# Compressing the cached chunks inside the state-space quarters, with chunks transposed as gathered and 64-row products

## What is computed

```python
def compress(rows, pos, w1, w2):
    ...
    chunks = rows[:, :nch * CMP_STRIDE].reshape(b, nch, CMP_STRIDE, g, dh)
    w1b = w1.reshape(r, CMP_STRIDE, dh, w1.shape[-1])
    hid = jnp.einsum('ld,ldh->h', pos, w1.reshape(CMP_LEN, dh, w1.shape[-1]))
    for j in range(r):
        hid = hid + jnp.einsum('bnsgd,sdh->bngh', chunks[:, j:j + nc], w1b[j])
    return jnp.einsum('bngh,hd->bngd', jax.nn.gelu(hid), w2)
```

## Time and profile before

| what | us |
|---|---|
| median of three runs | 3692.41 |
| the profiled execution: its own time / its span | 3694.21 / 3692.4 |
| the four S5 quarters, 285.5 to 528.1 | 242.6 |
| compression of the samples, 1110.4 to 1360.0 | 249.6 |
| head norm of the compressed keys, 1360.0 to 1378.6 | 18.6 |
| move to DRAM, 1047.9 to 1055.2 | 7.3 |

### The profile page before, as it was taken

The page is one execution under the profiler, slowest core; times in us unless marked ns, Lnnn a source line. Parts: engine busy times, 40 slices in busy tenths (PEclk is TensorE's granted clock), DMA queues, the critical chain, the costliest instruction groups (busy, mean ns, idle before and its releaser), DMA issues. The chain is left out here.

```text
span 3692.4 us, 51281 instructions
## 1 busy us (share of the span) xinstructions
PE 3078.9 (83%) x19609; PEld 2920.3 (79%) x19609; DVE 1562.7 (42%) x3343; ACT 947.6 (26%) x1636; POOL 711.1 (19%) x492
## 2 busy tenths in 40 slices
PE   6894336499966974799999999996587999999999
PEld 3894224499955862699999999994576999999998
DVE  5236656167732343334414334326564343243341
ACT  3211013255512430231201111312463311111111
POOL 2210003121100011132222222325221322222221
PEclk7996656579977986699999999996698999999999
DMA  2211110300025316211111111110101111111112
GB/s 95 56 30 39 37 43 13 107 1 1 1 92 194 138 47 137 62 46 46 46 46 46 47 51 44 47 42 0 36 1 48 42 47 50 46 45 46 46 45 71
DMA packets 272919, 191.66 MB, mean 52 GB/s; under 512 B 60612, under 2 KB 264494, under 8 KB 268639
## 3 DMA queue, kind: packets, MB, share of 16 engines
q1 hardware_dynamic: 267414, 139.86, 13.2%
q0 software_dynamic: 4608, 49.29, 4.3%
q10 hardware_dynamic: 733, 0.30, 0.0%
HBM read 171.37 MB, written 22.26 MB: 52 GB/s over the span
## 5 line engine op out<-in xcount | busy, mean ns | idle before, releaser
L551 PE MATMUL ps<-xf_hi,w_hi 128*128 128x344 f32 x2352 | 756.7, 322 | 9.9 <-POOL w_lo L542 9.9
L553 PE MATMUL ps<-xf_hi,w_lo 128*128 128x344 f32 x2352 | 753.2, 320 | 0.0
L552 PE MATMUL ps<-xf_lo,w_hi 128*128 128x344 f32 x2352 | 752.5, 320 | 0.0
L542 POOL TENSOR_TENSOR w_lo<-w_raw,w_hi 128x1024 fp32r<-128x1024 f32 (+1 forms) x162 | 384.7, 2375 | 1488.1 <-ACT w_hi L538 1488.1
L551 PEld LDWEIGHTS ps<-xf_hi,w_hi 128*128 128x128 f32 x2352 | 443.6, 189 | 11.3 <-issue 11.2
L552 PEld LDWEIGHTS ps<-xf_lo,w_hi 128*128 128x128 f32 x2352 | 443.5, 189 | 0.7 <-issue 0.7
L553 PEld LDWEIGHTS ps<-xf_hi,w_lo 128*128 128x128 f32 x2352 | 443.5, 189 | 0.0
L551 PE MATMUL ps<-hid_hi,w_hi 128*128 128x344 f32 x1056 | 339.4, 321 | 0.0
L553 PE MATMUL ps<-hid_hi,w_lo 128*128 128x344 f32 x1056 | 337.6, 320 | 0.0
L552 PE MATMUL ps<-hid_lo,w_hi 128*128 128x344 f32 x1056 | 336.9, 319 | 0.0
L538 ACT CAST w_hi<-w_raw 128x1024 fp32r<-128x1024 f32 (+1 forms) x162 | 165.7, 1023 | 387.1 <-PE ps L553 383.8
(11 more groups left out here) (531 smaller groups left out, 5626.1 us busy)
## 6 DMA issues: line engine op xcount, KB each, us to landing
w_raw<-in_ffn_w_up_dram SPq DMA_DIRECT2D x44, 512.0 KB
w_raw<-in_ffn_w_gate_dram SPq DMA_DIRECT2D x44, 512.0 KB, 3.7
w_raw<-in_ffn_w_down_dram SPq DMA_DIRECT2D x32, 448.0 KB, 3.6
w_raw<-in_ffn_w_down_dram SPq DMA_DIRECT2D x16, 512.0 KB, 3.8
w_raw<-in_a_w_in_dram SPq DMA_DIRECT2D x14, 512.0 KB, 3.6
w_raw<-in_c_w_in_dram SPq DMA_DIRECT2D x10, 512.0 KB, 3.9
xt<-in_x_prompt_dram SPq DMA_DIRECT2D x8, 512.0 KB
win_rows<-in_cache_nsa_win_dram SPq DMA_DIRECT2D x8, 512.0 KB
```

Source lines behind the costliest of these rows:

```text
L542: pool.tensor_tensor(self.parts.lo[:, slot, 0:kt, :], self.raw[:, slot, 0:kt, :], self.parts.hi[:, slot, 0:kt, :].bitcast(F32), ALU.subtra ...
L551: pe.matmul(psum, w_hi, x_hi, start=(a == 0), stop=False)
L552: pe.matmul(psum, w_hi, x_lo, start=False, stop=False)
L553: ins = pe.matmul(psum, w_lo, x_hi, start=False, stop=(a == kt - 1))
```

## The change

The four quarters and the compression become one stage, `stage_s5_compress`: four quarters of 32 steps. A step transposes four 128x128 pieces of a gathered chunk as they lie (both groups in one piece, group 0 on rows 0 to 63, group 1 on rows 64 to 127), and then multiplies the pieces of the step before: eight products, each on its group's 64 rows, the two halves alternating. The pieces of S5 on PE stand at fixed steps (`AT`), in two PSUM banks of their own. The regroup copies are gone; ACT copies all transposed chunks. The gathers are 32 of 1 MB, the first two issued at the end of `stage_linear`. The turns of the next quarter are made by DVE within the quarter before, those of the first at the start of the stage.

For the space, `hT` is stored to DRAM during `stage_linear` and brought back in `stage_window_sample`, in place of the attention's output; the weight `w1g` is loaded during `stage_linear` where hT was, serves both compressions, and the layouts w1s and w1p go. The position term (32 products before, 64 now) moves to the start of the stage. `stage_index` moves ahead of the projection. The head norm of the compressed keys joins the first head norm; gates, `stage_cmp_sample` and `stage_select` move ahead of `stage_rows`, which now waits for its stores at its end.

```diff
@@ stage_linear, S5Params @@
+                    if side and m == 4:
+                        side.sync_later(sp)
...
+                if side:
+                    side.gpsimd_last(pool)
...
+        self.cin.spill(sp)
         sp.wait_ge(s_b, 80)
@@ stage_rows @@
-                if not first:
-                    sp.wait_ge(s_store, 16 * len(stores))
+                sp.wait_ge(s_store, 16 * len(stores))
+class CompressInputs:
...
+    def spill(self, sp):
+        sp.dma_start(self.k.d_h, self.k.hT[:, :, :].rearrange("p f t -> p (f t)")).then_inc(self.s_spill, 16)
...
+    def gather(self, pool, v):
+        b, h, half = v // 4, v // 2 % 2, v % 2
+        pool.indirect_dma_start(self.X[v % NXC][:, :], None, self.table,
+                                bass.IndirectOffsetOnAxis(ap=self.idx[:, h, half, b:b + 1], axis=0)).then_inc(self.s_in[v % NXC], 16)
...
+AT = dict(Q0=1, Q1=2, KM=3, Q2=4, Q3=5, SEC_ODD=7, X0=9, X1=10, X2=11, XS0=12, XS1=13, Y0=18, Y1=19, YS=20, SEC_EVEN=25)
+STEPS = 32
@@ stage_s5_quarter becomes stage_s5_compress: PE @@
+                def products(n):
...
+                    pe.wait_ge(s_xT, n + 1)
+                    for a in range(4):
+                        for g in range(2):
+                            rows = slice(g * HD, (g + 1) * HD)
+                            ins = pe.matmul(sums(2 * kv + g)[:, h * P:(h + 1) * P], w1g[rows, kv, 8 * half + 4 * four + a, :],
+                                            xT[rows, n % NXT, a, :], start=(half == 0 and four == 0 and a == 0),
+                                            stop=(half == 1 and four == 1 and a == 3))
...
+                for q in range(n_q):
+                    for m in range(STEPS):
+                        n = q * STEPS + m
+                        transposes(n)
+                        if n:
+                            products(n - 1)
+                        for name in at_step(m):
+                            if (name, q) in where:
+                                other(name, q)
@@ ACT @@
+                        act.copy(xT[:, n % NXT, :, :], k.ps[:, n % 2, :].rearrange("p (a n) -> p a n", a=4)).then_inc(s_xT, 1)
+                        if n % 16 == 0 and n:
+                            half_sums(n // 16 - 1)
+                        if q and m == 0:
+                            by_step(q)
+                        if m == AT["SEC_EVEN"] - 1:
+                            gelu(2 * q)
+                        if q and m == AT["SEC_ODD"] - 1:
+                            gelu(2 * q - 1)
@@ DVE @@
+                turns(0)
+                for q in range(n_q):
...
+                    combine(V, r7, wb1, i7, wb2, ALU.add)
+                    dve.sem_inc(s_v, 1)
+                    if q:
+                        hidden(2 * q - 1)
...
+                    if q + 1 < n_q:
+                        turns(q + 1)
+                    hidden(2 * q)
+                    rows_out("SEC_EVEN", q)
@@ stage_window_sample @@
-                sp.dma_start(*move).then_inc(s_moved, 16)
+                sp.dma_start(k.hT[:, :, :].rearrange("p f t -> p (f t)"), k.d_h).then_inc(s_moved, 16)
```

More of the change, by code:

```diff
@@ L1027, in _, with stage_rows @@
                     pool.tensor_tensor(t, t, root[:, j % 4, 0:w], ALU.mult).then_inc(s_done, 1)
-def stage_rows(k, kv, tok, stok, stores, first=None):
+def stage_rows(k, kv, tok, stok, stores):
     nc = k.nc
@@ L1777, in stage_s5_quarter, with at_step, stage_s5_compress, bank @@
+AT = dict(Q0=1, Q1=2, KM=3, Q2=4, Q3=5, SEC_ODD=7, X0=9, X1=10, X2=11, XS0=12, XS1=13, Y0=18, Y1=19, YS=20, SEC_EVEN=25)
+STEPS = 32
+def at_step(n):
+    return [name for name, step in AT.items() if step == n]
+def stage_s5_compress(k, s, uT, cin, posb, kc, vc):
     nc = k.nc
-    g0 = qd * QG
     NU = NC + NB
+    n_q = 4
+    n_units = 4 * NB
+    names = list(AT)
+    others = [(name, q) for q in range(n_q) for name in names if not (name == "SEC_ODD" and q == 0)] + [("SEC_ODD", n_q)]
+    where = {x: n for n, x in enumerate(others)}
+    by_act = [name[0] in "QY" or name == "KM" for name, _ in others]
+    def bank(name, q):
+        return k.ps[:, 6 + where[name, q] % 2, :]
+    def done(name, q):
+        return where[name, q] + 1
+    def out_count(n):
+        return sum(1 for m in range(n + 1) if by_act[m] == by_act[n])
+    def copied(name, q):
+        return out_count(where[name, q])
@@ L1795, in stage_s5_quarter @@
[L1795 to L1799, removed]
+        ys = k.at("y_samples", [CG, QG, NB], k.h_at + (2 * 16 * P + 2 * 8 * 4 * HD) * 4)
@@ L1815, in _ @@
[L1815 to L1851, removed]
@@ new lines, in _, with half_sums @@
+                act.wait_ge(s_hz, 1)
+                def half_sums(b):
+                    for x in range(4):
+                        act.wait_ge(s_us, 16 * b + 12 + 2 * (x // 2) + 2)
+                        if b:
+                            act.wait_ge(s_hid, 4 * (b - 1) + x + 1)
+                            act.wait_ge(s_w2, 2 * b)
+                        act.copy(h1s[:, x, :], sums(x)[HD:P, 1:256]).then_inc(s_h1, 1)
+                        act.copy(hid[:, x, 0:255], sums(x)[0:HD, 0:255]).then_inc(s_h1, 1)
@@ new lines, in gelu, with other @@
+                def gelu(b):
+                    for x in range(4):
+                        act.wait_ge(s_hid, 4 * b + x + 1)
+                        if b == 0 and x == 0:
+                            act.wait_ge(s_posb, 1)
+                        act.activation(hid[:, x, :], hid[:, x, :], ACT.Gelu_apprx_tanh,
+                                       bias=posb[:, x // 2:x // 2 + 1]).then_inc(s_gelu, 1)
+                def other(name, q):
+                    n = where[name, q]
+                    if not by_act[n]:
+                        return
+                    src = bank(name, q)
+                    act.wait_ge(s_ps, n + 1)
+                    if name in ("Q0", "Q1", "Q2", "Q3"):
+                        x = int(name[1])
+                        dst = (Q, Q2)[x // 2][:, 4 * (x % 2):4 * (x % 2) + 4, :]
+                        if q and x < 2:
+                            act.wait_ge(s_g, q)
+                        ins = act.copy(dst, src.rearrange("p (g m) -> p g m", g=4))
+                    elif name == "KM":
+                        if q:
+                            act.wait_ge(s_T, 16 * 36 * q)
+                        ins = act.copy(km[:, :], src[:, 0:P])
+                    elif name == "YS":
+                        ins = act.copy(ys[:, :, :], src[0:CG, 0:QG * NB].rearrange("p (g b) -> p g b", b=NB))
+                    else:
+                        x = int(name[1])
+                        ins = act.copy(Y[:, 4 * x:4 * x + 4, :], src.rearrange("p (g n) -> p g n", g=4))
+                    ins.then_inc(s_free_a, 1)
@@ new lines, in by_step @@
+                def by_step(q):
+                    if q:
+                        act.wait_ge(s_fin, q)
+                    act.copy(ur[:, :, :], uT[:, q, 0:T].rearrange("p (n j) -> p j n", j=L)).then_inc(s_ur, 1)
+                by_step(0)
+                for q in range(n_q):
+                    for m in range(STEPS):
+                        n = q * STEPS + m
+                        act.wait_ge(s_tr, n + 1)
+                        if n >= NXT:
+                            act.wait_ge(s_us, n - NXT + 1)
+                        act.copy(xT[:, n % NXT, :, :], k.ps[:, n % 2, :].rearrange("p (a n) -> p a n", a=4)).then_inc(s_xT, 1)
[7 more added lines that the diff above has]
+                            gelu(2 * q - 1)
+                        for name in at_step(m):
+                            if (name, q) in where:
+                                other(name, q)
@@ L1853, in _ @@
+                half_sums(NB - 1)
+                gelu(NB - 1)
             @block.vector
@@ L1873, in _ @@
[L1873 to L1885, removed]
@@ new lines, in turns @@
+                def turns(q):
+                    g0 = q * QG
+                    link(dve.memset(cos[:, :, 0:1], 1.0))
+                    link(dve.memset(sin[:, :, 0:1], 0.0))
+                    for level in range(7):
+                        m = 2 ** level
+                        cc, cs = (bc(s.turns[:, level, n, g0:g0 + 1], [[1, QG], [0, m]]) for n in (0, 1))
+                        lo_c, lo_s, tmp = cos[:, :, 0:m], sin[:, :, 0:m], t1[:, :, 0:m]
+                        hi_c, hi_s = cos[:, :, m:2 * m], sin[:, :, m:2 * m]
+                        link(dve.tensor_tensor(hi_c, lo_c, cc, ALU.mult))
+                        link(dve.tensor_tensor(tmp, lo_s, cs, ALU.mult))
+                        link(dve.tensor_tensor(hi_c, hi_c, tmp, ALU.subtract))
+                        link(dve.tensor_tensor(hi_s, lo_c, cs, ALU.mult))
+                        link(dve.tensor_tensor(tmp, lo_s, cc, ALU.mult))
+                        link(dve.tensor_tensor(hi_s, hi_s, tmp, ALU.add))
@@ L1966, in stage_s5_states @@
+                hidden(NB - 1)
+                rows_out("SEC_ODD", n_q)
 def stage_s5_states(k, s):
```

(16 more changed lines are left out.)

604 lines of the change are left out of this document (288 added, 316 removed).

## The result

The changed kernel takes 3512.88 us, median of four runs (3508.92 to 3518.85), against 3689.76 us for the kernel before in four runs: a ratio of 0.9523, 95% interval 0.9502 to 0.9544. The forecast was 3535 us, 3482 to 3625. The profiled execution has a span of 3511.5 us and a mean granted clock of 0.904 (0.877 before).

What follows compares the result with a forecast made beforehand. A chain bounds the mixer's quarters, PE most of the compression, one after the other: 492 us. Merged, 94 + 3 x 74 + 10 + 8 = 334 us, 158 less; the rest about +1: 3535 us, range 3482 to 3625.

Steps and rivals of the forecast that it cites:

- The direction and the place: Whole kernel: 157 us less, with 158 us less in the merged stage and about 1 us more elsewhere.
- One step: Merged stage on PE: 1.33 us of work plus 0.23 for two mode changes, 1.56 us a step.
- a full drain: Mode changes on PE: 0.17 us twice a step, 1.68 us instead of 1.56, 15 us more over 128 steps.
- The waits for ACT: Each quarter, PE waiting for ACT: 3.5 us at the start, 2 in the middle, 2 at gelus, together 7.5.
- The 17 us for the mixer's pieces: Each quarter on PE: mixer's records 12.4 us, with second products, YS and mode changes 17 us.
- Start and tail: Merged stage's ends: 26 us until PE can pass its second step, about 10 us behind the last step.
- The 8 us for a cold clock: Merged stage after PE's first wait: 8 us added, as eight records take 2.08 us cold, 0.89 warm.
- The chain fits: Mixer's chain within a 74 us quarter: fits, with 4 us to spare at Y and 6 at the end.
- The rest: Outside the merged stage: -5.4 head norm, -1.4 move, +5.5 stage_rows, +2 projection and barrier, about +1 us.
- the slow clock's rival: Merged stage: clock stays low, steps take 3.1 us, stage 587 us, 3790 us in all; chance 0.06.

Runs made afterwards that it cites:

- two-step experiment: Changed kernel with two steps' transposes, then two steps' products, halving the changes between 128 and 64 rows: 3513.18 us.
- the mixer alone: Changed kernel without the chunk steps in the merged stage, the samples' compression result set to zero: stage 234.7 us, single run.
- both kernels with two steps: Changed kernel with two steps at a time, 3513.18 us; the same with ACT's copy by time step at the end of the quarter before, 3488.55 us.
- the early copy with single steps: Changed kernel with only ACT's copy by time step moved to the end of the quarter before: 3503.93 us.
- all together: Changed kernel plus two steps at a time, early copy, V ahead of the first turns, stage_rows' stores issued and waited for in the next stage: 3440.34 us.
- the one with the halves in turn: Changed kernel with a step's eight products run group 0 first, then group 1, instead of alternating: 3607.47 us, single run.

## Why the prediction was right, step by step

- **The direction and the place** were right: 157 us were forecast, 177 came, nearly all in the merged stage (324.1 us, 334 forecast). That a quarter came out so near, 73.8 to 75.5 us against 74, is luck in part: two errors of some 4 us each, in the steps and in the waits, cancel in it.
- **One step** was too cheap, 1.68 against 1.56 us, and so the term was 15 us too small over 128 steps. I had read a mode change off one interval on each side of it. In the changed kernel not one start is late behind each change but two: by 0.09 and 0.10 us into 64 rows (pairs of records) and by 0.09 and 0.05 us back. The two-step experiment confirms 0.35 us per step. That is what a full drain was worked out to be. The Trainium skill (TensorEngine Tiling (Array Packing), Key Properties), by which a change of mode drains the engine, was the better guide here. The size agrees with it; that the engine drains is not shown, as the ends of matmuls in the trace are modelled.
- **The waits for ACT** were too dear: 7.5 us a quarter forecast, while PE was idle for 3.3 us of the second quarter and 3.4 of the third. In the second quarter it lost 2.4 us at the start (3.5 forecast) and 0.9 in the middle (2), and nothing at the gelus (2). The 17 us for the mixer's pieces were right: 73.8 less 53.8 for the steps and 3.3 for the waits leaves 16.7.
- **Start and tail**: the first Q started 23.8 us into the stage (26 forecast) and the tail took 7.8 us (10). The 8 us for a cold clock were counted beside a wait that held most of them already: from 315.4 us, the end of that wait, to the quarter's end the granted clock was 0.97. The 2.08 and 0.89 us that they were read from are not alike, busy time with latency and a pace; 1.06 us is the busy time of the same records at full clock.
- **The chain fits** was right, with less slack than the 4 us at Y: the two-step experiment used it up.
- **The rest**: the head norm gained 5.2 us (50.0 + 18.4 became 63.2; 5.4 forecast); stage_rows and the prompt's compression lost 3.3 (67.4 became 70.7; 5.5 forecast), through the wait named; the projection stayed at 190 us, so the spill and the weights were hidden. By its own sum the slow clock's rival is 3788 us, not 3790.
- **Not forecast**: the prompt's attention, whose instructions the change does not touch, took 316.2 instead of 325.2 us. That is 9 of the 22 us by which the time came out below the forecast; the merged stage's 10 are most of the others.

## What to carry to other kernels

Two pieces of work that need nothing of each other, one bound by a chain and one by PE, are worth interleaving by hand: 156 us of the shorter one's 235 us disappeared, though the other's steps got slower. Before counting the steps' price, look for the switches (row mode, waits of the copying engine) that interleaving multiplies, and batch them. When a gain in PE's order does not show up, look at which small DMA now goes out next to a large one, and start the small chain a few steps earlier: here that sufficed, although the collision stayed.

## What the runs showed of the hardware

- Products on the two row halves ran in pairs at the pace of single ones when the halves alternated (1.09 us for 16 records) and mostly one after the other when they did not (1.64 us).
- A small store that goes out behind a gather of 1 MB is waited for longer. In the second to fourth quarters of every run that has the mixer, SP went on 2.4 to 2.5 us after the second store was issued where no gather had gone out in the 7 us ahead of the stores (the kernel before, the mixer alone, all kernels with single steps and the late copy), and 5.5 to 8.0 us after it where one had gone out 0.7 to 2.5 us ahead (both kernels with two steps, the early copy with single steps, all together). By what means the gather delays the store was not tried.
- The time at which the granted clock rises in the prompt's attention moves between kernels that run the same instructions there, and it is worth up to 12 us (316.2 to 328.6 us for that stage). Its stretch at 0.50 and the rest, of the kernel before, the changed one and the one with the halves in turn:

```profile
722.80:783.30 60.50, 53.34 (x255) 52.28 (x256) 27.78 (x135) 28.59 (x76) 17.58 (x30) 0.50 0.06 18
783.30:1048.00 264.70, 258.92 (x2066) 244.13 (x2066) 191.86 (x639) 142.08 (x273) 36.36 (x62) 1.00 0.01 1
```

```profile
857.30:895.70 38.40, 30.85 (x148) 29.80 (x149) 17.46 (x91) 19.88 (x53) 14.03 (x25) 0.50 0.10 28
895.70:1173.50 277.80, 272.06 (x2174) 256.39 (x2172) 201.66 (x682) 150.57 (x296) 40.05 (x68) 1.00 0.01 1
```

```profile
941.20:1010.80 69.60, 62.36 (x297) 61.12 (x297) 32.36 (x155) 32.10 (x85) 18.51 (x32) 0.50 0.06 16
```

PE has done 255, 148 and 297 records there when the clock rises, so no one place in the stage's work sets it. In the kernel with all changes it rose after 60.7 us again (324.9 us for the attention), so the 9 us are no property of the change. What sets the moment was not tried and stays open.
